# Row projections of a hybrid decoder step with the activations stationary: 128 tokens against 512 weight columns

## The chip, the cores and the metric

The kernel runs on one core of one Trainium2 chip. The metric is device time in microseconds, and smaller is better. TensorE is called PE in the profile, VectorE DVE, ScalarE ACT, GpSimd POOL, and SyncE SP; SP issues the large loads here. PEld is PE's weight load, the step that puts the stationary operand into the array.

## The reference

The program is one inference step of a two-layer decoder. It works on 512 prompt tokens and 64 sample tokens (8 sequences of 8), which share all weights, so the kernel treats them as one matrix of 576 tokens with 1024 features. Cut to what matters here, one layer does this:

```python
h = rms_norm(x, norm1_g) @ w_in                     # (T, 1024) @ (1024, N_IN)
q, k, v, qi, ki, wi, gq, gk, gv, ga, gr, gate_a, gate_b = jnp.split(h, offs, axis=-1)
q = partial_rope(rms_norm(q.reshape(B, T, 8, 64), q_g), pos, 16)
k = partial_rope(rms_norm(k.reshape(B, T, 4, 64), k_g), pos, 16)
qi = partial_rope(qi.reshape(B, T, 4, 64), pos, 16)
ki = partial_rope(rms_norm(ki, kidx_g)[:, :, None, :], pos, 16)[:, :, 0, :]
log_a = jax.nn.log_sigmoid((ga @ gla_wa2 + gla_ba)) / 16
attn_o = dsa_attention(q, qi, wi, pos, ki, topk, ...)   # index scores, top-k, attention over the chosen keys
gla_o, state = gla_recurrence(gq, gk, gv, log_a, s0)    # gated linear attention
x = merge_and_ffn(x, attn_o, gla_o, gr, gate_a, gate_b, ...)
```

The columns of the parts are q 512, k 256, v 256, qi 256, ki 64, wi 4, gq 256, gk 256, gv 512, ga 16, gr 512 and two gates of 1024. Everything is float32.

## The kernel before

**Numbers.** A float32 product is made of three passes in the 32-bit format fp32r. Each operand is split into a high part, which is a rounded copy, and a low part, which is the difference. The product is hi·hi + hi·lo + lo·hi, summed in PSUM. The activations `x_t` (features on partitions, 576 tokens along the row, 8 k tiles) are split into `in_hi` by ACT and `in_lo` by DVE (L2497). The norm's gain goes in there; its 1/rms is applied when a product leaves PSUM.

**Panels.** The weights come in panels of 128 columns by 1024 rows, 512 KB. SP loads them into a ring `w_raw` of three, three panels ahead (`load_panel`). ACT copies a panel to `w_hi` (L1889), and POOL subtracts to get `w_lo` (L1790); both have two buffers, and both wait until PE has finished the panel before the last. On PE (`part`) the weights are stationary and the activations move as two halves of 288 columns. A panel has 8 k tiles of 6 matmuls, 48 in all (L1352). Its output, 128 features by 576 tokens, fills two of the four banks of `prod`, so the next panel has the other two.

**Rows.** Attention and the gated linear attention need q, k, v, the index parts and gv with tokens on partitions (`q_rows`, `kv_rows`, `gv_rows`). These are 15 of the panels of each layer: 4 q, 2 k, 2 v, 2 qi, misc (ga, ki and wi together) and 4 gv; the list `STAGED` names their kinds. For each, ACT copies the product from PSUM to `stage` (L1972). After the first k tile of the next panel, PE turns it: four transposes of 128 tokens (L1465) and one of the 64 sample tokens (L1468) into two banks of `aux`. DVE takes them from there and multiplies them by `r_rows`, the 1/rms of each token (L2530 for q, with its heads put into another order, L2545 and L2553 for the rest). For misc, DVE first takes the 16 rows of ga out of PSUM into `ga_t` (L2307).

**The order.** A class `Plan` writes one list of steps. Every engine walks this list and does what is its own of each step, so its queue stands in that order. In `build_layer` the panels q to misc come first. The normalisations `qn` of q, k and the index keys (one step for each part and each of the five token tiles) are woven in after k tiles 3 and 6 of the panels from k to the first qi. In a `qn` step ACT squares, DVE sums (L2562), ACT forms the root, and DVE scales, applies the gain and rotates (L2258 to L2270). Then come gq and gk, with the items "z" (the decay projection from `ga_t`, ten small products, L1479), "z_min" (ACT's passes for the log-sigmoid) and "decay" woven in by `woven`; then gv with the first index scores and the top-k rounds, and then gr, the gates, the output projections and the feed-forward part, whose products are made by a scheme of seven block products for eight.

**The ends of a layer.** The last panels of layer 1 (`down`) are added to `x_t` by DVE (L2349 scales, L2351 adds). The first panel of layer 2 follows on PE directly.

**The start.** SP loads the x tiles, the gains and then three panels. ACT squares the rows of x and forms `r_rows` from them (L1871 to L1880) before it does anything else. Then it copies the first weights and makes the first `in_hi`. 

```python
for p in range(base, first["gq"]):
    self.start(p)
    for i in range(KD):
        self.add("part", p, i)
        if i == 0 and p > base:
            self.row(p - 1)
        if first["k"] <= p < first["qi"] + 1 and i in (3, 6) and len(normed) > NTILE:
            self.extra_step(normed.pop(0)[0])
```

## Time and profile before

| what | value |
|---|---|
| device time, three runs | 1836.33 us (median), 1833.85, 1837.96 |
| span of the profiled execution | 1837.1 us (no other time of that execution is given) |
| busy share of the span | PE 96%, PEld 92%, DVE 59%, ACT 43%, POOL 43% |
| HBM traffic | 149 MB, 81 GB/s over the span |
| panels | 79 per layer |

Times in the rows are in us from the start of the span unless marked ns. The busy time of a group of matmuls adds up durations that overlap, since the next matmul begins before the last has left the array; so starts are compared here rather than durations. In a timeline, "x4" is a run of four instructions of one line and kind, and a bracket tells how long the engine idled before it and who released it. A granted clock (PEclk) of 1.00 is TensorE's full speed.

### The profile page before, as it was taken

The numbers are of one execution on the slowest core, as the hardware profiler recorded it, in microseconds if no ns is written. First come the engines' busy times: TensorE is split into PE (matmuls) and PEld (weight loads), VectorE is DVE, ScalarE is ACT, GpSimd is POOL, SyncE is SP. The second block draws the span as 40 slices with busy tenths as digits, with TensorE's granted clock in tenths as the row PEclk, the third lists the DMA queues.
The fourth block names the chain that finished last, engine by engine and source line by source line (L and its number), as shares of the span: only waits on it lengthen the run. The fifth ranks groups of instructions, "written<-read, shape, count | busy, mean of one in ns | idle before, by whom it ended". The sixth has DMA issues, their size and how long they took to land.

```text
span 1837.1 us, 34731 instructions
## 1 busy us (share of the span) xinstructions
PE 1764.5 (96%) x13422; PEld 1685.4 (92%) x13422; DVE 1090.8 (59%) x2154; ACT 793.2 (43%) x1515; POOL 785.9 (43%) x508
## 2 busy tenths in 40 slices
PE   7998999999999999999999999999999999999998
PEld 7997888788999999999999878877899999999998
DVE  4655786355587537637536658744556874474463
ACT  4443214465466426426433422145645663363352
POOL 2322443342447447536333333425234563574452
PEclk9999999999999999999999999999999999999999
DMA  5232225214223413313222222342143234233122
GB/s 154 70 87 58 52 73 143 70 36 115 81 81 93 115 58 102 110 50 87 61 70 70 72 74 60 82 126 60 44 119 104 59 93 115 69 94 104 51 63 78
DMA packets 285711, 151.53 MB, mean 82 GB/s; under 512 B 17831, under 2 KB 284139, under 8 KB 285547
## 3 DMA queue, kind: packets, MB, share of 16 engines
q1 hardware_dynamic: 285546, 149.30, 29.7%
q8 instruction: 108, 1.77, 0.4%
q14 instruction: 57, 0.46, 0.1%
HBM read 141.89 MB, written 7.37 MB: 81 GB/s over the span
## 4 chain that ended last, share of the span: by engine, by line
PE 75%; DVE 15%; issue 3%; ACT 3%; SPq 2%; DMA 1%; POOL 0%; DVEq 0%; ACTq 0%; POOLq 0%
PE prod L1352 41%; PE prod L1406 8%; PE prod L1408 8%; PE prod L1407 8%; DVE scores L2710 2%; DVE top L2708 1%; PE aux L1765 1%; PE aux L1753 1%; PE aux L1465 1%; SPq L1179 1%; DVE in_lo L2247 1%; SPq L1185 1%; PE aux L1526 1%; PE aux L1728 1%; DVE aux L2480 1%
## 5 line engine op out<-in xcount | busy, mean ns | idle before, releaser
L1790 POOL TENSOR_TENSOR w_lo<-w_raw,w_hi 128x1024 fp32r<-128x1024 f32 (+1 forms) x158 | 370.8, 2347 | 757.6 <-ACT w_hi L1889 753.1
L1352 PE MATMUL prod<-in_hi,w_hi 128*128 128x288 f32 x1504 | 345.0, 311 | 12.8 <-DVE in_lo L2247 7.8
L1352 PE MATMUL prod<-in_lo,w_hi 128*128 128x288 f32 x1504 | 327.4, 300 | 0.0
L1352 PE MATMUL prod<-in_hi,w_lo 128*128 128x288 f32 x1504 | 326.1, 299 | 0.0
L1352 PEld LDWEIGHTS prod<-in_hi,w_hi 128*128 128x128 f32 x1504 | 244.8, 193 | 33.0 <-issue 24.6
L1889 ACT ACTIVATE w_hi<-w_raw 128x1024 fp32r<-128x1024 f32 (+1 forms) x158 | 163.1, 1032 | 246.1 <-PE prod L1352 245.8
L1352 PEld LDWEIGHTS prod<-in_lo,w_hi 128*128 128x128 f32 x1504 | 247.4, 193 | 0.0
L1352 PEld LDWEIGHTS prod<-in_hi,w_lo 128*128 128x128 f32 x1504 | 247.2, 192 | 0.0
L1406 PE MATMUL prod<-t_hi,ff_hi 128*128 128x288 f32 x704 | 208.7, 296 | 1.5 <-ACT in_sum L1941 0.7
L1352 PE MATMUL prod<-mid_hi,w_hi 128*128 128x288 f32 x960 | 207.6, 298 | 2.0 <-DVE mid_lo L2247 2.0
L1407 PE MATMUL prod<-t_lo,ff_hi 128*128 128x288 f32 x704 | 207.8, 295 | 0.0
L1408 PE MATMUL prod<-t_hi,ff_lo 128*128 128x288 f32 x704 | 207.1, 294 | 0.0
L1352 PE MATMUL prod<-mid_lo,w_hi 128*128 128x288 f32 x960 | 206.4, 296 | 0.0
L1352 PE MATMUL prod<-mid_hi,w_lo 128*128 128x288 f32 x960 | 206.3, 296 | 0.0
L1802 POOL TENSOR_TENSOR ff_lo<-ff_sum,ff_hi 128x512 fp32r<-128x512 f32 x88 | 127.4, 1451 | 80.6 <-ACT ff_hi L1937 80.6
L1352 PEld LDWEIGHTS prod<-mid_hi,w_hi 128*128 128x128 f32 x960 | 153.7, 188 | 3.5 <-DVE mid_lo L2247 3.5
L1406 PE MATMUL prod<-in_hi,ff_hi 128*128 128x288 f32 x528 | 156.4, 296 | 0.4 <-issue 0.4
L1408 PE MATMUL prod<-in_hi,ff_lo 128*128 128x288 f32 x528 | 155.3, 294 | 0.0
L1407 PE MATMUL prod<-in_lo,ff_hi 128*128 128x288 f32 x528 | 155.2, 294 | 0.0
L1352 PEld LDWEIGHTS prod<-mid_hi,w_lo 128*128 128x128 f32 x960 | 154.0, 188 | 0.0
L1352 PEld LDWEIGHTS prod<-mid_lo,w_hi 128*128 128x128 f32 x960 | 153.8, 188 | 0.0
L1406 PEld LDWEIGHTS prod<-t_hi,ff_hi 128*128 128x128 f32 x704 | 131.9, 187 | 3.2 <-issue 2.0
(316 smaller groups left out, 3213.5 us busy)
## 6 DMA issues: line engine op xcount, KB each, us to landing
w_raw<-in_w_in SPq DMA_DIRECT2D x76, 512.0 KB, 3.8
ff_gate<-in_w_ffn_gu SPq DMA_DIRECT2D x44, 512.0 KB, 5.2
ff_up<-in_w_ffn_gu SPq DMA_DIRECT2D x44, 512.0 KB, 4.0
w_raw<-in_w_ffn_down SPq DMA_DIRECT2D x32, 512.0 KB, 4.1
w_raw<-in_w_o SPq DMA_DIRECT2D x16, 512.0 KB, 3.9
w_raw<-in_w_ffn_down SPq DMA_DIRECT2D x16, 384.0 KB, 3.4
k_pages<-in_cache_k SPq DMA_DIRECT2D x32, 128.0 KB, 2.0
v_pages<-in_cache_v SPq DMA_DIRECT2D x32, 128.0 KB, 2.0
```

The costliest lines, as they stand in the source:

```text
L1179: return e.value_load(pages[0:1, i:i + 1], min_val=0, max_val=N_POOL - 1)
L1185: e.dma_start(dst[:, b % 4, n, :], src.rearrange("a s f -> (a s) f")).then_inc(sem[b % 4], 16)
L1352: ins = e.matmul(slot(g)[:, h, :], w[:, slot_w, i * P:(i + 1) * P], a[:, i, h * HALF:(h + 1) * HALF], start=first, stop=last)
L1406: e.matmul(out, ff_hi[:, q % FF_SLOTS, w], hi, start=first, stop=False, skip_group_check=True)
L1407: e.matmul(out, ff_hi[:, q % FF_SLOTS, w], lo, start=False, stop=False, skip_group_check=True)
L1408: ins = e.matmul(out, ff_lo[:, q % FF_SLOTS, w], hi, start=False, stop=(k == 3), skip_group_check=True)
L1465: ins = e.transpose(aux[:, bx, t * P:(t + 1) * P], stage[:, use % 2, t * P:(t + 1) * P], ident)
L1526: ins = e.matmul(aux[:, bank(key), 0:L], qi_t[rows, h // 2, j * P:(j + 1) * P], ki_t[rows, 0:L], start=True, stop=True)
L1790: e.tensor_tensor(w_lo[:, p % 2, 0:n], w_raw[:, p % RAW_RING, 0:n], w_hi[:, p % 2, 0:n].bitcast(F32), ALU.subtract).then_inc(w_lo_done, 1)
L1802: e.tensor_tensor(ff_lo[:, q % FF_SLOTS, :], ff_weights(name, b), ff_hi[:, q % FF_SLOTS, :].bitcast(F32), ALU.subtract).then_inc(ff_lo_don ...
L1889: e.activation(w_hi[:, p % 2, 0:n], w_raw[:, p % RAW_RING, 0:n], ACT.Copy).then_inc(w_hi_done, 1)
L2710: e.match_replace(out=buf, in_to_replace=t8[0:buf.shape[0], :], in_values=buf, imm_value=TAKEN).then_inc(dve_step, 1)
```

## The change

Four new kinds of panel take the place of the 15: `rq` (q, 512 columns), `rkv` (k and v, 512), `rqi` (qi, ki, wi and ga, 340) and `rgv` (gv, 512). Each kind has four panels, and each panel holds two k tiles of all the kind's columns. On PE 128 tokens of `in_hi` or `in_lo` are stationary and the weights move. The outputs have tokens on partitions at once. Token tiles 0 to 3 take the four banks of `prod`, all of them for one kind. The 64 sample tokens have their high and low parts side by side in a new operand `s_both` (128 columns), which moves past no extra pass: one matmul of `s_both` against the high weights and one of the 64 high columns alone against the low weights, into a bank of `aux`. The lower half of that bank's partitions is added to the upper half afterwards.

```diff
+ROW_PARTS = {"rq": [(O_Q, ATTN_W, 0)], "rkv": [(O_K, 2 * KV_W, 0)],
+             "rqi": [(O_QI, IDX_ROW_W + IDX_HEADS, 0), (O_GA, RANK, IDX_ROW_W + IDX_HEADS)],
+             "rgv": [(O_GV, GV_W, 0)]}
+ROW_W = {kind: sum(w for _, w, _ in parts) for kind, parts in ROW_PARTS.items()}
+ROWS = tuple(ROW_PARTS)
...
-    for kind, off, n in (("q", O_Q, 4), ("k", O_K, 2), ("v", O_V, 2), ("qi", O_QI, 2)):
+    def rows(kind):
+        return [(kind, i, [("w_in", 2 * i * P, 2, off, w, place) for off, w, place in ROW_PARTS[kind]])
+                for i in range(4)]
+
+    out += rows("rq") + rows("rkv") + rows("rqi")
...
+    out += rows("rgv")
+    for kind, off, n in (("gr", O_GR, 4), ("gta", O_GTA, 8), ("gtb", O_GTB, 8)):
         out += [(kind, i, [("w_in", 0, KD, off + i * P, P, 0)]) for i in range(n)]
```

PE's part of it, and what it waits for (in `part`, a kind of `ROWS` goes to `row_part`):

```diff
+                def row_part(p, i):
+
+                    kind, idx, _ = PANELS[p]
+                    t, kt, width = i % 4, 2 * idx + i // 4, ROW_W[kind]
+                    g, bank_t = plan.groups[p][t // 2], row_bank(p, t)
+                    cols = slice(i // 4 * width, (i // 4 + 1) * width)
+                    hi_w, lo_w = w_hi[:, p % 2, cols], w_lo[:, p % 2, cols]
+                    first, last = kt == 0, kt == KD - 1
+                    if first and g >= 2:
+                        if PANELS[p - 1][0] in ROWS:
+                            e.wait_ge(rows_out[t], row_no(kind) - 1)
+                        elif t % 2 == 0:
+                            e.wait_ge(free(("g", g - 2)), emptied(("g", g - 2)))
+                    if kind == "rq" and t == 0:
+                        e.wait_ge(split_lo, split_no(("norm", 1, kt)) + 1)
+                    tok = token_slice(t)
+                    out = bank_t[:, 0:width]
+                    e.matmul(out, in_hi[:, kt, tok], hi_w, start=first, stop=False)
+                    e.matmul(out, in_hi[:, kt, tok], lo_w, start=False, stop=False)
+                    ins = e.matmul(out, in_lo[:, kt, tok], hi_w, start=False, stop=last)
+                    if last:
+                        ins.then_inc(row_ready[t], 1)
+                    if t < 3:
+                        return
+                    key = ("rs", kind)
+                    if first:
+                        e.wait_ge(free(key), opened(key))
+                    if kind == "rq":
+                        e.wait_ge(sample_lo, nth(kt + 1, KD))
+
+                    e.matmul(aux[:, bank(key), 0:width], s_both[:, kt, :], hi_w, start=first, stop=False,
+                             skip_group_check=True)
+                    ins = e.matmul(aux[0:NS, bank(key), 0:width], s_both[:, kt, 0:NS], lo_w, start=False,
+                                   stop=last, skip_group_check=True)
+                    if last:
+                        ins.then_inc(ready(key), 1)
+                    elif i == KD - 1:
+                        ins.then_inc(row_part_done, 1)
```

The outputs leave PSUM scaled: tiles 2 and 3 by ACT, which also copies the lower half of the sample bank, and tiles 0 and 1 by DVE, which adds the sample halves and scales them. ACT:

```diff
+                        if kind_p in ROWS:
+                            if kind_p == "rq":
+                                e.wait_ge(r_rows_done, nth(1, 1))
+                                if layer:
+                                    e.wait_ge(stored, nth(0, 16 * 3 * NTILE))
+                            for t in (2, 3):
+                                e.wait_ge(row_ready[t], row_no(kind_p))
+                                for src, dst in row_dests(kind_p, t):
+                                    ins = e.activation(dst, src(row_bank(p, t)), ACT.Copy, scale=r_rows[:, t:t + 1])
+                                ins.then_inc(rows_out[t], 1)
+                            key = ("rs", kind_p)
+                            dst = stage_slot(("fold", kind_p))
                             e.wait_ge(ready(key), filled(key))
-                            if kind_p == "misc":
-                                e.wait_ge(ga_done, nth(1, 1))
-                            e.activation(halves(dst), src, ACT.Copy).then_inc(staged, 1)
+                            e.activation(dst[0:NS, 0:ROW_W[kind_p]], aux[NS:P, bank(key), 0:ROW_W[kind_p]],
+                                         ACT.Copy).then_inc(staged, 1)
```

DVE:

```diff
+                        if kind_p in ROWS:
+                            if kind_p == "rq" and layer:
+                                e.wait_ge(stored, nth(0, 16 * 3 * NTILE))
+                            for t in (0, 1):
+                                e.wait_ge(row_ready[t], row_no(kind_p))
+                                for ps, dst in row_dests(kind_p, t):
+                                    ins = e.tensor_scalar(dst, ps(row_bank(p, t)), r_rows[:, t:t + 1], None, ALU.mult)
+                                ins.then_inc(rows_out[t], 1)
+                            key = ("rs", kind_p)
+                            use = stage_no(("fold", kind_p))
+                            e.wait_ge(staged, use + 1)
+                            for ps, dst in row_dests(kind_p, 4):
+                                ins = e.tensor_tensor(dst, ps(aux[0:NS, bank(key), :]), ps(stage[0:NS, use % 2, :]), ALU.add)
+                            ins.then_inc(free(key), 1)
+                            e.wait_ge(free(key), emptied(key))
+                            dests = [dst for _, dst in row_dests(kind_p, 4)]
+                            if kind_p == "rq":
+                                dests = [q_rows[0:NS, 4, 0:ATTN_W]]
+                            for dst in dests:
+                                ins = e.tensor_scalar(dst, dst, r_rows[0:NS, 4:5], None, ALU.mult)
+                            ins.then_inc(rows_out[4], 1)
```

The staging, the `row` steps with their transposes and DVE's work on them are gone, and so is ga from PSUM; in its place a step `gaT` transposes the 16 columns of ga in five parts, with one copy for the prompt and one for the samples. The `z` items come one item later. The norms' places move too:

```diff
         for p in range(base, first["gq"]):
             self.start(p)
+            if p == 0:
+                self.add("xstat")
             for i in range(KD):
                 self.add("part", p, i)
-                if i == 0 and p > base:
-                    self.row(p - 1)
-                if first["k"] <= p < first["qi"] + 1 and i in (3, 6) and len(normed) > NTILE:
+                if p < first["rqi"]:
+                    due = 2 * NTILE
+                else:
+                    due = NTILE
+                if p >= first["rkv"] and i in (2, 6) and len(normed) > due:
                     self.extra_step(normed.pop(0)[0])
-            if p == base:
+            if p == base + 1:
                 self.rstd(1)
             self.finish(p)
         assert len(normed) == NTILE
 
-        items = [[], normed[0] + [("z",)], [("z_min",)] + normed[1], normed[2], [("decay",)], [("decay_ref",)] + normed[3],
+        items = [[], normed[0] + [("gaT",)], [("z",)] + normed[1], [("z_min",)] + normed[2], [("decay",)],
+                 [("decay_ref",)] + normed[3],
                  normed[4], [("qkT", 0)], [("qkT", 1), ("decay_exp",)], [("qn_end",), ("qkT", 2)], [("qkT", 3)],
                  [("qkT", 4)]]
-        self.woven(range(first["gq"], first["gv"]), items)
...
+                    elif kind == "gaT":
+                        for i in range(2):
+                            e.wait_ge(free(("gaT", i)), opened(("gaT", i)))
+                            for t in range(4 * i, min(4 * i + 4, NTILE)):
+                                n = tile_rows(t)
+                                e.wait_ge(rows_out[t], row_no("rqi"))
+                                ins = e.transpose(aux[0:RANK, bank(("gaT", i)), t % 4 * P:t % 4 * P + n],
+                                                  wga_rows[0:n, t, IDX_HEADS:WGA_W], ident[0:n, 0:n])
+                            ins.then_inc(ready(("gaT", i)), 1)
```

`s_both` is made with the splits for the first norm, by one small instruction more on ACT and one on DVE for each k tile:

```diff
+                        if norm == 1:
+                            e.activation(s_both[:, kt, 0:NS], x_t[:, kt, SEQ:NT], ACT.Copy,
+                                         scale=gains[:, layer, gain:gain + 1]).then_inc(sample_hi, 1)
...
+                        if norm == 1:
+                            e.wait_ge(sample_hi, nth(kt + 1, KD))
+                            e.scalar_tensor_tensor(out=s_both[:, kt, NS:2 * NS], in0=x_t[:, kt, SEQ:NT], scalar=scale,
+                                                   in1=s_both[:, kt, 0:NS].bitcast(F32), op0=ALU.mult,
+                                                   op1=ALU.subtract).then_inc(sample_lo, 1)
```

ACT and POOL wait for the panel before the last by a function `panel_done`, which for the first three panels of a kind is a semaphore of its own, and they work on `panel_cols(p)` columns (1024, in `rqi` 680). A panel of `rqi` is loaded by two DMAs. The squares of x and `r_rows` are now a step `xstat`, which stands in ACT's queue behind the first splits and the first two weight copies, unchanged in itself; `rstd(1)` follows panel 1 in place of panel 0. The loads of the start come in another order:

```diff
             for t in range(NTILE):
                 src = A["x_prompt"][0, t * P:(t + 1) * P, :] if t < 4 else A["x_sample"].rearrange("b s d -> (b s) d")
                 e.dma_start(x_rows[0:tile_rows(t), t, :], src).then_inc(x_loaded[t], 16)
-                if t == 3:
+                if t == 0:
                     load_gains(0)
-            for p in range(RAW_RING):
+                if t == 1:
+                    load_panel(0)
+            for p in range(1, RAW_RING):
                 load_panel(p)
```

## Rows read from the trace of the kernel before

**Rows 1.** Page, part 1: busy us, share of the span, instructions, by engine

```profile
PE 1764.5 (96%) x13422; PEld 1685.4 (92%) x13422; DVE 1090.8 (59%) x2154; ACT 793.2 (43%) x1515; POOL 785.9 (43%) x508
```

**Rows 2.** Page, part 4: the chain that ended last, by engine

```profile
PE 75%; DVE 15%; issue 3%; ACT 3%; SPq 2%; DMA 1%; POOL 0%; DVEq 0%; ACTq 0%; POOLq 0%
```

**Rows 3.** Timeline of PE, two panel boundaries: start us, us, operation

```profile
44.59 0.66 PE L1465 MATMUL aux<-cst,stage 128*128 128x128 f32 x4
...
45.11 0.52 PE L1352 MATMUL prod<-in_hi,w_hi 128*128 128x288 f32 x2
...
51.04 0.42 PE L1352 MATMUL prod<-in_lo,w_hi 128*128 128x288 f32 x2
51.30 0.43 PE L1352 MATMUL prod<-in_hi,w_lo 128*128 128x288 f32 x2
51.73 0.65 PE L1465 MATMUL aux<-cst,stage 128*128 128x128 f32 x4
```

**Rows 4.** Waits of PE: who waited for whom, us in total, times, longest

```profile
PE aux L1465 <- ACT stage L1972: 3.6, 6, 0.9
```

**Rows 5.** Timeline of PE in attention: products of 384 and 512 columns

```profile
383.31 0.33 PE L1368 MATMUL aux<-k_lo,q_split 128*128 128x384 f32 x1
383.48 0.43 PE L1352 MATMUL prod<-in_hi,w_hi 128*128 128x288 f32 x2
...
411.14 0.39 PE L1368 MATMUL aux<-k_lo,q_split 128*128 128x512 f32 x1
411.37 0.42 PE L1352 MATMUL prod<-in_hi,w_hi 128*128 128x288 f32 x2
```

**Rows 6.** Timeline of PE: outputs of 64 partitions, a row transpose and score sums

```profile
45.08 0.27 PE L1468 MATMUL aux<-cst,stage 128*64 128x128 f32 x1
...
184.38 0.43 PE L1352 MATMUL prod<-in_hi,w_lo 128*128 128x288 f32 x2
184.74 1.29 PE L1563 MATMUL aux<-s_heads,cst 128*64 128x320 f32 x4
185.96 0.53 PE L1352 MATMUL prod<-in_hi,w_hi 128*128 128x288 f32 x2
```

**Rows 7.** One line's instructions (ns min/median/max); timeline of DVE

```profile
L1889 ACT ACTIVATE w_hi<-w_raw x158: 839/1052/1067, 14.6 to 1820.5; 128x1024 fp32r<-128x1024 f32 x142, 128x768 fp32r<-128x768 f32 x16
...
59.64 0.69 DVE L2545 TENSOR_TENSOR kv_rows<-aux,r_rows 128x512 f32<-128x512 f32 x1 [0.42 <-PE aux L1465]
```

**Rows 8.** Timelines of DVE and POOL, normalisation of q beside a weight subtraction

```profile
59.85 2.41 POOL L1790 TENSOR_TENSOR w_lo<-w_raw,w_hi 128x1024 fp32r<-128x1024 f32 x1 [4.73 <-ACT w_hi L1889]
...
61.35 1.47 DVE L2258 TENSOR_TENSOR q_rows<-q_rows,sums 128x512 f32<-128x512 f32 x1
...
65.10 0.68 DVE L2258 TENSOR_TENSOR q_rows<-q_rows,sums 128x512 f32<-128x512 f32 x1
```

**Rows 9.** Timelines of PE and DVE where gq begins

```profile
103.53 0.50 PE L1352 MATMUL prod<-in_hi,w_hi 128*128 128x288 f32 x2
...
105.28 2.56 PE L1479 MATMUL aux<-wa,ga_t 17*128 17x256 f32 x10
...
107.56 0.22 DVE L2270 TENSOR_TENSOR kv_rows<-rope,rope 64x64 f32<-64x64 f32 x1
```

**Rows 10.** Timelines of PE and DVE where the second layer begins

```profile
921.71 0.43 PE L1352 MATMUL prod<-in_hi,w_hi 128*128 128x288 f32 x2
...
922.84 0.76 DVE L2351 TENSOR_TENSOR x_t<-prod,x_t 128x576 f32<-128x576 f32 x1
```

**Rows 11.** Chain in order of time, the last two steps of the start

```profile
16.44 2.28 DVE in_lo L2497
...
18.86 1.30 PE prod L1352 x4
```

**Rows 12.** Stretches: us, busy of PE, PEld, DVE, ACT, POOL, clock, DMA share, GB/s

```profile
0.00:17.40 17.40, 7.28 (x41) 6.29 (x41) 7.21 (x14) 10.50 (x19) 1.86 (x5) 1.00 0.96 268
17.40:24.30 6.90, 5.44 (x23) 5.47 (x24) 6.90 (x7) 4.54 (x7) 2.98 (x2) 0.51 0.42 114
```

223 lines of the change are left out of this document (98 added, 125 removed).

## The prediction, made before the changed kernel was run

> **What bounds the kernel now.** I read the page first. TensorE is busy for 1764.5 us of the span and holds 75% of the chain that ended last; DVE, next, holds 15% [rows 1, 2]. So a microsecond comes off the kernel only where TensorE's stream gets shorter or where a wait of that stream goes. The timeline of PE then shows what one input panel costs: from the row transposes at 44.59 us to the next ones at 51.73 us are 7.14 us, of which the block of five transposes takes 0.52 (45.11 less 44.59) and 48 matmuls of 288 columns the rest, 0.138 each on the mean and 0.133 from start to start inside the stream (two in 0.265) [rows 3]. The durations of 0.3 us are no guide: they overlap. The list of waits shows that those transposes wait for ACT's staging copy 3.6 us in all, six times [rows 4]. The other engines idle beside this stream most of the time.
>
> **The change, part by part.** All times come from the profiled execution, whose span is 1837.1 us; that is 0.8 above the median of the three runs shown, so I take the difference off the median.
>
> *The stream.* Removed per layer: 15 panels (4 q, 2 k, 2 v, 2 index, misc, 4 gv) of 7.14 us, 107.1 us, transposes included. Added per layer: four kinds of four panels with 8 x 3 prompt matmuls and 2 x 2 sample matmuls, 28 each; twelve panels are 512 columns wide, the four of the index kind 340. The trace has three-pass operands at 512 columns in the attention logits: the second of such a pair starts 0.23 us before the next matmul (411.14 to 411.37), with 384 columns 0.17 us [rows 5]. I take 0.23 (ends 0.22 and 0.24, since the rows are rounded) and for 340 columns, between 0.133 and 0.17, 0.155. That is 336 x 0.23 + 112 x 0.155 = 94.6 us. Gain 12.5 per layer, **24.9 us** in all. With the low ends (0.22, 0.133) it is 37, with the high ones (0.24, 0.17) 15. The number of columns hardly changes (207,360 against 210,112 per layer); what goes is the fixed part of 272 matmuls and the 75 transposes.
>
> *Waits that go:* the 3.6 us of rows 4, since neither the staging nor the misc panel's product is between two panels any more. **3.6 us.**
>
> *The narrow stationary.* In each half panel the last sample matmul has 64 stationary columns, 64 such instructions in all. A plain matmul of that shape is costly to enter and leave: the last two of 288 columns before the score sums take 0.36 instead of 0.265, and the four of these with the return take 1.22, so about 0.09 each way [rows 6]. The fifth row transpose has 64 stationary columns too and costs nothing: its start is 0.49 after the first of four and the next matmul starts 0.03 later [rows 6]. The dtype of the new ones is that of neither. I take nothing, as they stand amid equal matmuls like the transposes, and keep 64 x 0.18 = 11.5 us as the other end. The Trainium skill (TensorEngine Tiling (Array Packing), Key Properties) says that changing the tiling mode drains TensorE, which speaks against this change; the first pair of rows 6 agrees with it and by it the sum would be 11.5 us worse. The same skill (PSUM — Partial Sum Buffer, on the zero region) says that float32r matmuls force the full column group, by which nothing would be drained; no run so far shows it.
>
> *Ga by transposes.* Five transposes per layer, 0.13 each by the block of rows 3: **+1.1 us**. The z products wait for DVE's copies of them. After the index kind ends (0), ACT evicts its two tiles and folds (to 1.0), casts the next weights (1.05, to 2.1), and POOL subtracts (2.4, to 4.5) [rows 7, 8]. DVE meanwhile has the last k tile's norm. Such an operation of two SBUF operands takes 1.47 us while POOL works on w_lo and 0.68 without it [rows 8], so the norm ends about 1.5 after POOL, at 6.0; it now ends 4.3 us after the row block (103.53 to 107.8) with a smaller load [rows 9]. The copies add 0.9 (the 128x512 move from PSUM is 0.69 [rows 7]), to 7.0. TensorE is there after five steps of 0.8 and the transposes, at 4.7, where the z block now begins without a wait [rows 9]. Stall 2.3 per layer, **+4.6** (0 to 8). What is late next is the chain of ACT's three passes over z; the decay products that need it stand two items later, six steps and the z block of 2.5 us behind [rows 9], and I count nothing for them.
>
> *Evictions.* All four banks of prod belong to one kind, so the next kind needs them at once. Tile 0's bank is complete 2.5 us before the kind ends, tile 3's 0.45, and the next kind comes to them in turn every 0.69 us. DVE's 0.69 (q's turned heads in two instructions of half the width) and the same on ACT, by estimate, fit: nothing on the path if DVE is free. It is: from one q norm's product to the next's are 3.75 us, of which 0.8 is what POOL's work costs it [rows 8]; with that in part of them, some 3.4 each, five q norms need 17 of the 25.8 us (112 x 0.23) of the kv kind. If DVE were late by a norm (3 us), each of eight boundaries could cost that.
>
> *Weights.* The w_hi copy (1.05) stands in ACT's queue behind evictions and the squares of the norms, and POOL's 2.4 follows [rows 7, 8]. A 512 panel lasts 6.4 us, so the copy may begin 2.9 us late; an index panel (680 columns in place of 1024) lasts 4.3 with 0.7 + 1.6 us of work, and may begin 2.0 us late. By walking ACT's queue I find only the third index panel late, by 0.6 per layer: **+1.2** (0 to 5). SP's queue issues four DMAs more per layer, three panels ahead, and waits for POOL there now: hidden.
>
> *The second layer's first panel* opens banks of both last down panels. The last addition to x begins at 922.84 and takes 0.76, to 923.60; the stream begins at 921.71 and comes to the third tile 1.38 later, at 923.09 [rows 10]: **+0.5**.
>
> *The start.* The x tiles' last landing waits for 512 KB of weights in front, 2 us at the rate of rows 12; against that ACT's squares and the first cast are out of the way and POOL's first w_lo is done, which now holds DVE's first in_lo for 2.28 us until TensorE starts at 18.86 [rows 11]. With the loads at 268 GB/s [rows 12] I get 18.0; until 24.3 the granted clock is 0.51, the 1.2 of TensorE's two levels of 1.2 and 2.4 GHz [rows 12], so half of it counts: **-0.5**. The squares now delay the third panel's weights until 35.5, where TensorE arrives at 35.4: nothing. Ends -1.5 and +1.5.
>
> Sum: -24.9 - 3.6 - 0.5 + 1.1 + 4.6 + 1.2 + 0.5 = **-21.6 us**, 1815.5 in the profile's terms, 1814.7 on the median.
>
> **Rivals.**
> - *Drain.* The narrow stationary costs like the plain one: 1814.7 + 11.5 = 1826. For it the score-sum rows, against it the transposes [rows 6]. Chance 0.17.
> - *Clean handover.* Neither the z wait nor the index weights bite, and a 340-column matmul costs nearer 0.145: 4.6 + 1.2 + 2.2 us more gain, 1807. For it: the walks above take every queue at its latest. Chance 0.13.
> - *Weights late, the other side.* ACT stands in the norms' handshakes with DVE, so that each weight cast of the kv and index kinds, 16 panels, starts behind them. It decides from 1.35 us of wait per panel (21.6/16); if the slack of 2.9 and 2.0 is exceeded by 3, TensorE loses 48 us: 1863. For it: the norms now come in two per 6.4 us instead of 7.14, and each costs up to 3.75 beside POOL's work [rows 8]. Against it: five q norms in 25.8 us leave room. Chance 0.04.
> - *Moved wait.* The stream is shorter but the gv stage is held by DVE's top-k and index work, and the stalls give all back: about 1836. DVE holds 15% of the chain [rows 2], though it idles between those steps. Chance 0.03.
> - The change does what it says; I see no way in which it would not.
>
> **Numbers.** Forecast 0.63, 1814.7, its own range 1808 to 1822. The range of 1804 to 1828 takes in the fast end of the stream partly, the clean handover and the drain, and leaves out the two last rivals. A stretch at half clock more or less, such as the 6.9 us of rows 12, costs half its length, 3.5 us, and lies inside it. A measurement of this kernel tells 0.2% (3.7 us) from no change. Faster by more: 0.63 + 0.17 + 0.13 = 0.93; within: 0.03; slower: 0.04.
>
> **What would show it.** In the profile after: 512-column groups at L1352's successor with 0.23 us from start to start; no staging or row transposes, a wait of about 2 us before the z products on DVE's ga copies, a short one on w_lo in the index panels, one before the third tile of the second layer. It would be wrong if the narrow matmuls' neighbours lie 0.3 us apart, if PE waits for POOL's w_lo at most panels, or if the four kinds' stages are not 77 and 17 us of stream per layer.

## The result, and the profile after

The changed kernel takes 1826.91 us, the median of six runs (1825.65 to 1833.26), beside 1836.39 for the kernel before in six (1833.85 to 1837.96). The ratio is 0.9955, with a 95% interval of 0.994 to 0.997. Two more sets of runs were made on other chips: 1830.41 beside 1835.52 (0.9976, 0.9962 to 0.9989) and 1830.42 beside 1836.36 (0.9963, 0.9949 to 0.9976). So the change gains 5 to 9.5 us. Forecast were 21.6, and 1814.7: the sign was right, the size not.

The profiled execution has a span of 1831.5 us; it is the slowest of the six (1833.26), so it shows less of the gain than the medians. The page (parts 1 and 4) answers to [rows 1, 2]:

```profile
PE 1747.9 (95%) x12738; PEld 1638.1 (89%) x12738; DVE 1099.6 (60%) x2146; ACT 796.6 (43%) x1535; POOL 784.0 (43%) x510
...
PE 73%; DVE 14%; ACT 4%; issue 3%; SPq 3%; DMA 2%; POOL 1%; DVEq 0%; ACTq 0%; POOLq 0%
```

PE is busy 16.6 us less (1764.5 less 1747.9), but the span is only 5.6 shorter. So 11.0 us of what was taken out of PE's work came back as time in which PE is not busy, and part of its busy time is work at a lower clock. The waits of PE (who waited for whom: us in total, times, longest) show new names:

```profile
PE aux L1785 <- DMA k_pages<-in_cache_k: 5.7, 3, 3.2
...
PE prod L1400 <- POOL w_lo L1891: 5.0, 5, 1.6
PE aux L1693 <- ACT gk_rows L2263: 4.5, 2, 2.2
...
PE aux L1581 <- DVE ga_t L2644: 3.2, 2, 1.6
...
PE aux L1589 <- DVE la L2676: 2.6, 2, 1.3
...
PE prod L1456 <- DVE wga_rows L2426: 1.0, 2, 0.5
```

In the kernel before, the first of them stood so:

```profile
PE aux L1683 <- DMA k_pages<-in_cache_k: 1.8, 2, 1.3
```

Where they fall is seen when the start of each kind's first product is read from PE's timeline. The table gives the length of each stretch in the two profiled executions:

| stretch | before, layer 1 | after | before, layer 2 | after |
|---|---|---|---|---|
| q (first product at 18.86, 18.89) | 31.91 | 29.91 | 32.51 | 28.63 |
| k and v | 28.96 | 25.55 | 28.96 | 25.55 |
| index parts and ga | 21.44 | 20.55 | 21.44 | 20.52 |
| gq and gk | 39.68 | 43.66 | 39.70 | 45.16 |
| gv | 49.19 | 45.17 | 47.65 | 45.26 |
| gr to the next layer, or the last down panels | 731.67 | 735.89 | 435.38 | 436.86 |

A kind's stream promises 4 x (7.14 - 6.39) = 3.0 us where 512 columns move, and the three such kinds gain 2.0 to 4.0. The index kind gains 0.9 where 3 x 7.14 less 4 x 4.39, 3.9, were in the stream. gq and gk, whose own panels are unchanged, take 4.0 and 5.5 us longer, and behind gr the kernel takes 4.2 and 1.5 us longer.

**The stream.** PE's timeline at full clock, with the narrow stationary of the samples in the middle, and inside an index panel:

```profile
30.90 0.39 PE L1413 MATMUL aux<-w_hi,s_both 128*128 128x512 f32 x1
31.13 0.40 PE L1415 MATMUL aux<-w_lo,s_both 128*64 128x512 f32 x1
31.36 0.39 PE L1400 MATMUL prod<-w_hi,in_hi 128*128 128x512 f32 x1
```

```profile
85.12 0.32 PE L1401 MATMUL prod<-w_lo,in_hi 128*128 128x340 f32 x1
85.27 0.32 PE L1402 MATMUL prod<-w_hi,in_lo 128*128 128x340 f32 x1
```

512 columns take 0.23 from start to start [rows 5], 340 take 0.15, and the one with 64 stationary columns takes 0.23 like its neighbours. A panel of 512 columns lasts 6.39 us, an index panel without waits 4.39, so a layer's stream is 12 x 6.39 + 4 x 4.39 = 94.2 us; forecast were 94.6.

**The index kind and gq.** PE's timeline again; a bracket is the idle time before, and who ended it:

```profile
84.86 0.42 PE L1400 MATMUL prod<-w_hi,in_hi 128*128 128x340 f32 x1 [1.62 <-POOL w_lo L1891]
...
89.80 0.43 PE L1400 MATMUL prod<-w_hi,in_hi 128*128 128x340 f32 x1 [0.34 <-POOL w_lo L1891]
...
94.90 0.50 PE L1456 MATMUL prod<-in_hi,w_hi 128*128 128x288 f32 x2 [0.50 <-DVE wga_rows L2426]
...
97.36 0.75 PE L1568 MATMUL aux<-cst,wga_rows 128*16 128x128 f32 x5
...
101.48 2.53 PE L1581 MATMUL aux<-wa,ga_t 17*128 17x256 f32 x10 [1.58 <-DVE ga_t L2644]
...
111.87 0.35 PE L1589 MATMUL aux<-cst,la 128*128 128x128 f32 x1 [1.34 <-DVE la L2676]
```

The same five waits stand in layer 2, within 0.07 us. The third is that of gq for the bank that DVE empties last. The last two, before z and before the decay products, stand where the kernel before has none.

**Why the weights are late.** First ACT, then POOL, then DVE around the beginning of the index kind (74.35):

```profile
78.26 0.42 ACT L2170 ACTIVATE sq_rows<-kv_rows 128x256 f32<-128x256 f32 x1 [2.21 <-DVE kv_rows L2439]
...
82.28 0.76 ACT L1992 ACTIVATE w_hi<-w_raw 128x680 fp32r<-128x680 f32 x1
```

```profile
76.13 1.66 POOL L1891 TENSOR_TENSOR w_lo<-w_raw,w_hi 128x680 fp32r<-128x680 f32 x1 [5.17 <-ACT w_hi L1992]
```

```profile
76.15 1.92 DVE L2439 TENSOR_SCALAR kv_rows<-kv_rows,r_rows 64x512 f32<-64x512 f32 x1
```

DVE scales the sample rows of k and v from 76.15 to 78.07, beside POOL's w_lo. Only then does ACT square the first tile of k (78.26): the first norm of a part waits for all five tiles of it, the samples' too. DVE is behind by one norm from there. ACT's queue holds the copy for the third index panel behind that norm, so it begins at 82.28, POOL follows it, and PE waits until 84.86. The same instruction costs a quarter elsewhere (ns, min/median/max):

```profile
L2439 DVE TENSOR_SCALAR kv_rows<-kv_rows,r_rows x2: 1921/1922/1924, 76.1 to 975.6; 64x512 f32<-64x512 f32 x2
...
L2439 DVE TENSOR_SCALAR gv_rows<-gv_rows,r_rows x2: 478/478/479, 185.5 to 1086.5; 64x512 f32<-64x512 f32 x2
```

For gv, with as many elements and with POOL idle when it starts (185.5; POOL's next work begins at 185.81), it takes 0.48; for k and v 1.92. The Trainium skill (SBUF — State Buffer, Who interferes with whom) says that only the port pair shared by DVE and GpSimd causes contention, and that it is an exclusive lock. The trace agrees: the two began 0.02 us apart, POOL's ended at its usual length (77.79), and DVE's 0.28 after it.

**Why z and the decay are late.** DVE in the gq stage, ACT at the end of its passes over z, and DVE in the kernel before:

```profile
97.21 1.90 DVE L2373 TENSOR_TENSOR kv_rows<-kv_rows,sums 64x256 f32<-64x256 f32 x1
...
100.30 0.93 DVE L2644 COPY ga_t<-aux 16x512 f32<-16x512 f32 x2
107.66 0.22 DVE L2653 TENSOR_REDUCE sums<-sq_rows 128x1 f32<-128x64 f32 x1 [6.43 <-ACT sq_rows L2170]
...
109.08 0.76 DVE L2443 SCALAR_TENSOR_TENSOR gq<-prod,rstd 128x576 f32<-128x576 f32 x1
109.75 1.86 DVE L2676 SCALAR_TENSOR_TENSOR la<-aux,la 128x512 f32<-128x512 f32 x3
```

```profile
107.32 0.24 ACT L2170 ACTIVATE sq_rows<-q_rows 128x64 f32<-128x64 f32 x1
```

```profile
110.52 1.87 DVE L2585 SCALAR_TENSOR_TENSOR la<-aux,la 128x512 f32<-128x512 f32 x3 [2.75 <-ACT la L2085]
```

The copies of ga stand behind the last norm of k, which POOL stretches again (1.90 for 0.41), so z waits 1.58. Then `z_min`, which writes `la`, has slipped behind two things on DVE, since z comes one item later and ahead of its item's norm: that norm, whose square ACT makes only after its passes over z, and gq's own product. DVE sits idle until that square, does the norm from 107.66, and takes gq's product at 109.08 without any wait for PE. So `la` comes at 109.75, 3.8 us after ACT began its last pass over z (105.95). In the kernel before it came 0.74 after (110.52 and 109.78), with the norm and gq's product behind it. PE waits 1.34 us before the decay products.

**The start.** ACT, DVE and PE, answering to [rows 11]:

```profile
17.03 0.78 ACT L2116 ACTIVATE in_hi<-x_t,gains 128x576 fp32r<-128x576 f32 x1 [6.34 <-DVE gains L2345]
...
24.29 1.05 ACT L1992 ACTIVATE w_hi<-w_raw 128x1024 fp32r<-128x1024 f32 x1
```

```profile
14.76 2.09 DVE L2352 COPY x_t<-aux 128x512 f32<-128x512 f32 x4 [0.58 <-PE aux L1375]
```

```profile
18.89 0.76 PE L1400 MATMUL prod<-w_hi,in_hi 128*128 128x512 f32 x1 [2.42 <-DVE in_lo L2626]
...
28.04 0.50 PE L1400 MATMUL prod<-w_hi,in_hi 128*128 128x512 f32 x1 [1.05 <-POOL w_lo L1891]
```

The last copies of x end at 16.85 (14.2 before): the 512 KB in front cost 2.7 us. The squares are out of the way and the first `in_lo` takes 0.82 instead of 2.28, so PE starts at 18.89, as before. But the second copy of weights now waits for eight splits of 0.92 us each, with the samples' own copies among them (0.68 before), and starts at 24.29 (20.90 before), and PE loses 1.05 at the second panel.

**The clock.** Where the z products stood idle and where the decay starts, the granted clock falls (us, busy of the five engines, clock, DMA share, GB/s):

```profile
100.00:103.90 3.90, 2.42 (x10) 1.59 (x10) 1.12 (x4) 1.01 (x2) 0.00 (x0) 1.00 0.42 129
103.90:107.40 3.50, 3.50 (x15) 3.46 (x15) 0.00 (x0) 3.44 (x9) 0.00 (x0) 0.51 0.00 0
1001.60:1008.50 6.90, 6.90 (x23) 5.18 (x23) 0.00 (x0) 4.61 (x10) 0.00 (x0) 0.51 0.00 0
```

Both stretches follow the 1.6 us wait; the kernel before has 1.00 in its z block (105.2 to 108.7). In the seven profiles that have the wait before z, such a stretch begins 0.6 to 3.6 us behind each of the 14 waits. The waits for weights in the index kind of layer 2 are as long (1.6), and none comes within 17 us of them. In all, 44.8 us of this execution are at 1.2 GHz instead of 2.4, against 38.0 before; in the two other profiles of the changed kernel it is 37.6 and 54.1.

### The profile page after: what moved, and what is told of

It reads as the page before. It is cut to its first block, busy times and chain, and to the rows that moved or that the text cites. A ratio compares the mean times of both kernels' runs of the same rounds, so it can differ in the third digit from the quotient of the medians.

```text
span 1831.5 us, 33285 instructions
## 1 busy us (share of the span) xinstructions
PE 1747.9 (95%) x12738; PEld 1638.1 (89%) x12738; DVE 1099.6 (60%) x2146; ACT 796.6 (43%) x1535; POOL 784.0 (43%) x510
## 4 chain that ended last, share of the span: by engine, by line
PE 73%; DVE 14%; ACT 4%; issue 3%; SPq 3%; DMA 2%; POOL 1%; DVEq 0%; ACTq 0%; POOLq 0%
PE prod L1456 32%; PE prod L1510 8%; PE prod L1511 8%; PE prod L1512 8%; PE prod L1400 2%; PE prod L1401 2%; PE prod L1402 2%; PE aux L1867 1%; PE aux L1855 1%; SPq L1244 1%; DVE scores L2801 1%; DVE in_lo L2362 1%; SPq L1250 1%; DVE top L2799 1%; PE aux L1628 1%
## 5 line engine op out<-in xcount | busy, mean ns | idle before, releaser
L1891 POOL TENSOR_TENSOR w_lo<-w_raw,w_hi 128x1024 fp32r<-128x1024 f32 (+2 forms) x160 | 370.1, 2313 | 752.7 <-ACT w_hi L1992 748.2
L1992 ACT ACTIVATE w_hi<-w_raw 128x1024 fp32r<-128x1024 f32 (+2 forms) x160 | 163.2, 1020 | 276.4 <-PE prod L1456 244.9
L1456 PE MATMUL prod<-in_hi,w_hi 128*128 128x288 f32 x1024 | 238.8, 315 | 8.8 <-DVE in_lo L2362 7.8
L1456 PE MATMUL prod<-in_lo,w_hi 128*128 128x288 f32 x1024 | 224.4, 302 | 0.0
L1456 PE MATMUL prod<-in_hi,w_lo 128*128 128x288 f32 x1024 | 224.1, 301 | 0.0
L1456 PEld LDWEIGHTS prod<-in_hi,w_hi 128*128 128x128 f32 x1024 | 169.4, 195 | 25.7 <-issue 17.6
L1456 PEld LDWEIGHTS prod<-in_lo,w_hi 128*128 128x128 f32 x1024 | 170.0, 195 | 0.0
L1456 PEld LDWEIGHTS prod<-in_hi,w_lo 128*128 128x128 f32 x1024 | 169.9, 194 | 0.0
```

Of the source, the lines that this page charges most:

```text
L1456: ins = e.matmul(slot(g)[:, h, :], w[:, slot_w, i * P:(i + 1) * P], a[:, i, h * HALF:(h + 1) * HALF], start=first, stop=last)
L1891: e.tensor_tensor(w_lo[:, p % 2, 0:n], w_raw[:, p % RAW_RING, 0:n], w_hi[:, p % 2, 0:n].bitcast(F32), ALU.subtract).then_inc(w_lo_done, 1)
L1992: e.activation(w_hi[:, p % 2, 0:n], w_raw[:, p % RAW_RING, 0:n], ACT.Copy).then_inc(w_hi_done, 1)
```

## The experiments

**The changed kernel again, twice** (no edit).

> The changed kernel again. Its six runs so far lie in two groups, 1825.7 to 1827.3 and 1832.4 to 1833.3, with mean granted clocks of 0.989 to 0.992 and 0.988. Theory A (the change gained some 16 us of stream and small waits, and half-clock stretches more or less make the groups): in the runs of this kernel a time about 5.5 us longer goes with a mean clock lower by 0.003, and the profile up to the start of gr again shows some 11 us less over both layers. Rival B (the stages behind gr wait for something that does not start earlier, such as the loads of the pages in SP's queue): the profile again has over 2 us of PE's wait on k_pages in layer 1, and the time stays near 1826 to 1833 whatever the clock.

> The changed kernel once more, on the chip of the two others, as their yardstick: 1824 to 1832, with a granted clock about 0.002 below that of the kernel before.

Measured: 1830.41 us in twelve runs and 1830.42 in six, with mean clocks of 0.9869 and 0.9865 beside 0.9895 and 0.9884 for the kernel before on the same chips. There are no two groups, but a spread of 1823 to 1835 that goes with the clock: the run at 0.992 took 1823.42, those at 0.983 and 0.984 took 1835.42 and 1835.23. Over all 24 runs of this kernel a line through time and clock falls by 1.0 us for 0.001, less than I had expected (5.5 for 0.003). By that line 0.002 to 0.0026 less clock go with 2 to 2.6 us. If all of a half-clock stretch cost half its length, 0.001 would be 1.8 us (3.7 us at 1.2 GHz); so part of it seems to fall where PE would have waited anyway. PE's wait on k_pages was 4.0 us in the second profile, 3.3 of them in layer 1, as the rival had it. As far as the start of gr, the two profiles lie 2.5 and 5.0 us ahead in layer 1, and 9.2 and 8.3 over both layers, not 11.

**The start undone**, wholly and in part. The first kernel puts the squares in front again and takes the old order of loads, the second the order alone:

```diff
-                if t == 0:
+                if t == 3:
                     load_gains(0)
-                if t == 1:
-                    load_panel(0)
-            for p in range(1, RAW_RING):
+            for p in range(RAW_RING):
                 load_panel(p)
```

> The squares of x stand in front again and the loads are in the old order; all else is the changed kernel. Theory A (the new start gains nothing: the x tiles land later behind 512 KB of weights, and the second w_hi copy stands behind 8 small sample splits): PE's first product at about 18.9 us or earlier, no wait on w_lo before panel 1, or less than 1.05 us, and the rq kind ends 0 to 2 us earlier. Rival (the start was a gain of 0.5 us, as forecast): the end of the rq kind comes 0.5 us or more later, since ACT's splits begin behind 5 us of squares.

> Only the order of the first loads is the old one, the squares stay behind the splits. Theory A: the last x tile's copies end 2 us earlier (14.3 instead of 16.8), the first w_hi copy (1.05) comes then, and POOL's first w_lo (2.35) takes DVE's first in_lo with it, so PE starts at about 18.0 and the rq kind ends 1 to 2 us earlier than 48.8. Rival: the weights, now last, land after 16.8 and PE starts later than 18.9.

Measured: 1827.64 and 1827.26 us, on the chip where the changed kernel took 1830.41. With both undone PE starts at 18.87 and the k kind at 47.73. With the order alone undone:

```profile
14.11 2.10 DVE L2624 SCALAR_TENSOR_TENSOR in_lo<-x_t,gains,in_hi 128x576 fp32r<-128x576 f32 x1 [0.99 <-ACT in_hi L2114]
```

```profile
16.35 0.76 PE L1398 MATMUL prod<-w_hi,in_hi 128*128 128x512 f32 x1 [3.69 <-DVE in_lo L2624]
```

PE starts at 16.35, with POOL's lock on the first `in_lo` (2.10) as expected but 1.6 earlier than expected, and the k kind begins at 45.40. There is no wait at the second panel. The start moves from one profile to the next, and other kernels of this document share it. With the new start (eight profiles) the k kind begins at 47.2 to 49.3, 48.3 on the mean; with the order alone undone (three) at 44.8 to 46.8, 45.7 on the mean. So the new order of the loads costs some 2.6 us, and moving the squares gains about 2 by the one profile without it (47.7). Whether both together gain or lose anything cannot be told. The medians are 3 us shorter, within the spread.

**The norms of k one panel later.**

```diff
-                if p >= first["rkv"] and i in (2, 6) and len(normed) > due:
+                if p >= first["rkv"] and p != first["rqi"] and i in (2, 6) and len(normed) > due:
```

> The norms of k leave the first index panel free and stand in the last three (five steps for six places). Theory A (w_lo of the third and fourth index panel is late, 1.62 and 0.34 us per layer, because ACT's copy stands behind norms of k which wait for DVE): the third panel's wait falls from 1.62 to under 0.5 us, the kind is 1 to 2 us shorter per layer, unless the norms crowd the fourth panel, and the time falls by 2 to 3 us. Rival B (what is gained before gr is lost behind it): the kind is shorter, but the time is within 1 us of the changed kernel's. Rival D (the number of norms in the kind counts, not their place): the wait moves to the last panel and to the first of gq and stays 2 us in all.

Measured: 1835.34 us, as slow as the kernel before (1.0, 0.9987 to 1.0013). The index kind lasts 21.6 us instead of 20.5, and gq and gk 47.2. The waits of PE:

```profile
PE prod L1456 <- DVE wga_rows L2426: 8.2, 2, 4.1
```

The waits for weights in the index kind are gone, as expected, but the gain did not come. The norms now crowd the kind's end, and DVE empties its last bank 4.1 us late per layer, where it was 0.5; the kind is 17.56 of stream and this wait. The rival that only the number of norms counts had the place but not the size, and the wait on `la` is 5.7 us as well. The mean clock is 0.984, as low as in any kernel.

**gaT ahead of the norm.**

```diff
-        items = [[], normed[0] + [("gaT",)], [("z",)] + normed[1], ...
+        items = [[], [("gaT",)] + normed[0], [("z",)] + normed[1], ...
```

> The gaT step stands before the first norm of its item, in place of behind it. Theory A (the z products wait 1.6 us per layer because DVE's copies of ga stand behind the last norm of k, which POOL's subtraction stretches): that wait goes, the ten z products start 1.6 us earlier relative to gq's start, and, since ACT's three passes over z start earlier too, the wait before the decay products (1.3 us per layer) does not grow. Gain 2 x 1.6 = 3.2 us, up to 5 if the half-clock stretch that follows that wait in each profile so far (at 103.95 and 1001.66) does not come. Rival (ACT's and DVE's norm chain sets the stage): the wait on la grows by what the z wait loses, and gq plus gk stay at about 43.7 us (layer 1) in time corrected for the clock.

Measured: 1829.83 us (0.9958, 0.9945 to 0.9971), no change that can be told. The changed kernel did not run on this chip, so the ratio to the kernel before is what compares. The wait before z is gone, and the wait on `la` has grown (DVE's timeline, then PE's waits):

```profile
107.43 0.76 DVE L2443 SCALAR_TENSOR_TENSOR gq<-prod,rstd 128x576 f32<-128x576 f32 x1
108.10 1.86 DVE L2676 SCALAR_TENSOR_TENSOR la<-aux,la 128x512 f32<-128x512 f32 x3
```

```profile
PE aux L1589 <- DVE la L2676: 5.7, 2, 2.9
```

The two waits were 3.2 + 2.6 us and are 0 + 5.7, so the rival holds in its waits. It is not a plain move, though. `la` again comes 3.8 us after ACT began its last pass over z, and with z earlier the decay products begin 15.3 us behind gq's start in both layers, where they began 17.0 and 18.5 behind. PE comes to them earlier still, since no half-clock stretch lies between z and them. So it seems that in the changed kernel the stretch fell on time that PE would otherwise have waited for `la`. gq and gk last 42.0 and 45.1 us (43.7 and 45.2 before the edit); in layer 2 a stretch at half clock comes right behind the wait on `la` instead.

**The sample rows scaled as they leave PSUM** (loops and semaphores are left out of the cut).

```diff
+    ins = e.tensor_scalar(dst, ps(aux[0:NS, bank(key), :]), r_rows[0:NS, 4:5], None, ALU.mult)
     e.wait_ge(staged, use + 1)
-    ins = e.tensor_tensor(dst, ps(aux[0:NS, bank(key), :]), ps(stage[0:NS, use % 2, :]), ALU.add)
-    ins = e.tensor_scalar(dst, dst, r_rows[0:NS, 4:5], None, ALU.mult)
+    ins = e.scalar_tensor_tensor(out=dst, in0=ps(stage[0:NS, use % 2, :]), scalar=r_rows[0:NS, 4:5],
+                                 in1=dst, op0=ALU.mult, op1=ALU.add)
```

> The sample rows are scaled as they leave PSUM, before ACT's fold is there, and the fold is scaled and added in one step; the scaling of SBUF by SBUF (1.92 us beside POOL's w_lo, 76.15 to 78.07 in the profile) is gone, as many instructions on DVE. Theory A (that stretched instruction holds the next norm, and the norm holds ACT's copy for the third index panel): the first norm of k starts 1.5 to 1.9 us earlier, the wait before the third index panel falls from 1.62 to about 0, the index kind lasts 18.0 to 19.0 us in place of 20.5; 2 to 4 us in all. Rival (the norms themselves are too slow for panels of 4.4 us): the wait moves to the fourth panel and the kind stays above 20 us.

Measured: 1826.82 us (0.9956, 0.9943 to 0.9969). DVE, and PE at the third and fourth index panel:

```profile
73.33 0.74 DVE L2433 TENSOR_SCALAR kv_rows<-aux,r_rows 64x512 f32<-64x512 f32 x1 [1.02 <-PE aux L1416]
74.31 0.74 DVE L2439 SCALAR_TENSOR_TENSOR kv_rows<-stage,r_rows,kv_rows 64x512 f32<-64x512 f32 x1 [0.23 <-ACT stage L2085]
```

```profile
82.28 0.43 PE L1401 MATMUL prod<-w_hi,in_hi 128*128 128x340 f32 x1 [0.34 <-POOL w_lo L1892]
...
87.22 0.43 PE L1401 MATMUL prod<-w_hi,in_hi 128*128 128x340 f32 x1 [0.34 <-POOL w_lo L1892]
```

The last step ends at 75.05, where POOL's work has just begun (74.92), and the wait at the third panel falls from 1.62 to 0.34 us. The index kind lasts 19.16 us, 1.4 less in each layer. The last step ends 1.9 us behind the kind before it instead of 3.7: 1.44 of these 1.8 are the stretching beside POOL, and the rest is that the scaling no longer waits for ACT's copy. So the stretched scaling was the main cause of the late weights, and 0.34 at two panels is what is left. In the time of the whole kernel this edit alone does not show: its ratio is that of the changed kernel (0.9955 to 0.9976 on other chips).

**The narrow stationary made wide.**

```diff
-    aux[0:NS, bank(key), 0:width], s_both[:, kt, 0:NS], lo_w
+    aux[:, bank(key), 0:width], s_both[:, kt, :], lo_w
```

> The second sample matmul has all 128 columns of s_both stationary in place of 64, so lo x lo of the samples is computed too and no matmul of these kinds is narrower than the others. Theory A (the 64-column stationary costs nothing: 0.23 us from its start to the next in the changed kernel's timeline, like its neighbours): the start-to-start times are the same within 0.01 us and the time is the changed kernel's within its noise of 4 us. Rival (drain, 0.18 us for each of 64): 11 us faster.

```profile
30.98 0.39 PE L1415 MATMUL aux<-w_lo,s_both 128*128 128x512 f32 x1
31.21 0.39 PE L1400 MATMUL prod<-w_hi,in_hi 128*128 128x512 f32 x1
```

Measured: 1828.03 us (0.9954, 0.9939 to 0.9968), and 0.23 from start to start, as before the edit. The drain rival is out. Of the two rules that the prediction weighed, that of the Trainium skill (PSUM — Partial Sum Buffer, The four PSUM rules) on float32r matmuls forcing the full column group agrees with this; the one on draining (TensorEngine Tiling (Array Packing), Key Properties) does not show at an fp32r matmul with 64 stationary columns among ones with 128.

**Four edits together, the decay one item later.** The sample rows scaled first, the old order of loads, gaT ahead, and:

```diff
-   [("z_min",)] + normed[2], [("decay",)], [("decay_ref",)] + normed[3], normed[4],
+   [("z_min",)] + normed[2], normed[3], [("decay",)], [("decay_ref",)] + normed[4],
```

> Four edits together: the loads of the start in the old order, gaT before the norm, the sample rows scaled first, and the decay products one item later (it now waits 1.3 us per layer for la). Theory A (each handover costs what its wait shows, and they are on the path): 2.5 (start) + 3.2 (z) + 2.6 (la) + 3.5 (index weights) = 11.8 us less than the changed kernel, of which a part may be given back as half-clock stretches; 1815 to 1820. Rival B (what comes before gr does not carry to the end): earlier by 8 us or more at gr of layer 1, but less than half of it left at the gates' second kind, and 1823 or more in the end.

Measured: 1831.42 us (0.997, 0.9959 to 0.9981), not the 1815 to 1820 expected, and not by the rival's way either: at gr of layer 1 it is 7.1 us ahead of the kernel before, not 8 or more. At the start of gq in layer 2 this kernel is 15.4 us ahead of the one before, but gq and gk last 46.7 and 45.5 us, 7 and 6 more than before:

```profile
PE aux L1602 <- ACT q_t L2178: 6.0, 2, 3.0
```

The decay's own work on DVE (`decay_ref` and what follows) now ends later, the norm behind it too, and behind that norm stand ACT's weight copy and its first copy of q, which PE waits for: 3.0 us per layer. A step moved back to where its input is ready pushed back the chain behind it.

**z_min ahead of gq's product**, and with it the best version.

```diff
-        items = [[], normed[0] + [("gaT",)], [("z",)] + normed[1], [("z_min",)] + normed[2], [("decay",)],
+        items = [[], [("gaT",)] + normed[0], [("z",), ("z_min",)] + normed[1], normed[2], [("decay",)],
```

> The changed kernel with two moves in the gq stage: gaT ahead of the norm of its item, and z_min directly behind z, so that on DVE it stands ahead of gq's product. Theory A (with gaT ahead alone the wait on la grew from 1.3 to 2.9 us per layer, since DVE's z_min stands behind gq's own product, which waits for PE): the waits before z and before the decay products, 2.9 us per layer in the changed kernel, are both under 0.5, and gq plus gk last about 40.8 us in layer 1 in place of 43.7; 1806 to 1809 us in time corrected for the clock means a gain of 5.8. Rival (something third takes over, ACT's passes or q_t's transposes): gq plus gk stay over 42.5 us.

> zmin_early with the old order of the first loads and the sample rows scaled as they leave PSUM. Theory A (the handovers are on the path): 5.8 (z, la) + 2.5 (start) + 2.8 (index weights) = 11 us less than the changed kernel on the same chip; some 1817 to 1820, less what goes back as half-clock stretches (4 to 7 us at the clocks seen so far). Rival B (gains before gr do not reach the end): under 3 us less than the changed kernel.

Measured: 1823.17 us (0.993, 0.9917 to 0.9943) and, with the old load order and the scaling in PSUM, 1819.06 us (0.9908, 0.9895 to 0.992), where the changed kernel took 1830.42 on the same chip. DVE's order is turned round:

```profile
96.41 0.93 DVE L2644 COPY ga_t<-aux 16x512 f32<-16x512 f32 x2 [1.43 <-PE aux L1568]
...
103.49 1.87 DVE L2676 SCALAR_TENSOR_TENSOR la<-aux,la 128x512 f32<-128x512 f32 x3 [4.42 <-ACT la L2200]
...
106.81 0.76 DVE L2443 SCALAR_TENSOR_TENSOR gq<-prod,rstd 128x576 f32<-128x576 f32 x1
```

```profile
PE aux L1604 <- ACT q_t L2180: 2.5, 2, 1.3
```

The waits before z and the decay are gone (5.8 us), and one of 1.3 us per layer on ACT's copy of q has come (2.5); gq and gk last 40.4 us in both layers. So the two moves in the plan gain 3.3 us by waits, and 7.2 by the runs. In the profiles gq and gk shrink by 3.3 and 4.8 us, of which the waits are 1.7 per layer; the rest fits half of the stretches of 3.4 and 6.8 us at half clock, of which this profile has none in the stage. The mean clock is 0.9892 instead of 0.9865, which at 1.0 us for 0.001 is 2.7 us. The best version lasts 11.4 us less than the changed kernel, against 11 expected, at a clock of 0.987. Theory A stands in its total: the handovers together cost about what their waits show, and what was taken away before gr did reach the end. Its check by time corrected for the clock (1806 to 1809) did not hold: the span less half of its 33.3 us at half clock is 1802.2, and the changed kernel's three profiles give 1801.8 to 1809.1 by the same sum. PE's waits for the weights of the row kinds, 5.0 us in the changed kernel, are down to this:

```profile
PE prod L1399 <- POOL w_lo L1890: 1.4, 4, 0.3
```

## Why the prediction was wrong in its size

The bound was read rightly, and so was the stream. The terms, both layers together, as the profiled execution has them:

| term | forecast | measured |
|---|---|---|
| stream, with the row transposes | -24.9 | -25.8 (2 x (107.1 - 94.2)) |
| waits for staging | -3.6 | -3.6 |
| narrow stationary | 0 | 0 |
| transposes of ga | +1.1 | +1.3 (2 x 0.65) |
| wait before z | +4.6 | +3.2 |
| wait before the decay products | 0 | +2.6 |
| weights of the index kind | +1.2 | +3.9 |
| gq's wait for the last bank | 0 | +1.0 |
| layer 2's first banks | +0.5 | +0.6 |
| the start | -0.5 | +1.1 (48.80 less 47.73), not clear of the spread |
| page loads (5.7 less 1.8) | 0 | +3.9, open |
| half clock (44.8 less 38.0, halved) | 0 | at most +3.4 |

The sum of the last column is -8.4. The profiles differ by 5.6, the medians by 9.5, 5.1 and 5.9. Of the 2.8 between, 1.5 are PE's wait on `gk_rows` (4.5 for 3.0; it is 3.0 in the two other profiles of this kernel), and the rest has no place. The last term and the wait on `la` overlap in part, by the run with gaT ahead.

- **"I count nothing for them"**, of the decay products, is the step that failed most plainly. I asked whether ACT's passes over z would be in time, and not what `z_min` would stand behind on DVE once z was an item later. It stands behind a norm and gq's product. Before, it began at 110.52 and gq's product at 113.85. That cost 2.6 us, and moving it back, with gaT, took 7.2 us off the kernel, part of it by the clock.
- **"By walking ACT's queue I find only the third index panel late, by 0.6"**: the place was right, the size 1.62 and 0.34 more at the fourth. The prediction had POOL's lock for the norms, 0.8 each, and left out the scaling of the sample rows, 1.44 longer beside POOL, right in front of ACT's square of the first tile of k.
- **"Nothing on the path if DVE is free. It is"**: at the end of the index kind it was late by 0.5 us, behind a norm of which one small step (L2381, 128x32) took 2.39 us beside POOL's w_lo at 90.77 and 0.18 at 87.80. At the other boundaries of a kind PE has no wait, as forecast.
- **The start**: the squares behind the splits gain about 2 us, and the loads' order loses some 2.6. I had the landing 2 us later (it was 2.7) and did not see that the second cast stands behind eight splits with an extra step each.
- **The z wait**: the mechanism was the one forecast (the norm stretched by POOL, 1.90 us), 1.6 in place of 2.3.
- **The clock** was held to be a matter of chance inside the range. It was lower in the changed kernel on both chips where it was compared, and as high as before (0.9892, 0.9884) in the kernel without the two waits. In the profiles every wait before z has a stretch behind it, and where z waits no more, the kernel with z_min ahead has no stretch in gq and gk, and the best version one of 3.4 us, in layer 2. That this wait brings the stretch is the likeliest reading; but the best version, which lacks both waits too, had 0.987, so the mean clock is not settled by it.

Of the rivals, the drain is out (the wide matmul); its price of 0.09 for each way was read too boldly, since rows 6 show the way in (0.36 for 0.265) but do not part the way back from the four matmuls themselves. Weights late was right in its mechanism, but at 4 of the 16 panels it named, and by less than 2 us each; its 48 us needed every panel. Even the best version stops at 17.3 us, short of the 21.6, with 0.3 at some panels, a clock 0.0014 lower than before and the page loads left.

The page loads stay open. SP issues them behind the end of the sample recurrence: 286.35 against 290.74 before, only 4.4 us earlier where PE was 6 ahead, and PE waited 3.18 for them at 311.11. From 286.35 to 314.8 SP issues them one behind the other with little idle time, so that its own pace sets when the last come. PE's wait was 3.6 to 6.2 us in every profile with the new panels and 1.8 before. From gr of layer 1 to the next layer each of these twelve profiles took 732.9 to 738.0 us, where the kernel before took 731.7, and in 2.2 to 3.7 of that PE waited for the pages (0.5 before); behind gr of layer 2 no such loss shows (740.3 to 747.1 to the end, 745.2 before). The sum had no term for this: it took what PE gains ahead of gr to be kept. That these loads keep their time while PE gets ahead is the reading of these rows; no run changed their order.

## What to carry to other kernels

When a plan is written by hand, a step that is moved has to be looked up in every queue: what stands between its old and its new place on each engine, and whether one of those waits for something that comes later still. Shorter panels leave the helpers less time, so an instruction that a shared port stretches fourfold is cheap in one stage and sets the next one's start in another; reading it from PSUM, before POOL's work began, took it off the path here. Two small waits in one stage cost more than their length when the clock falls behind them.

## What was not expected of the hardware

A scaling of 64 x 512 in SBUF took 1.92 us beside a POOL subtraction of 1.66, and 0.48 with POOL idle at its start. In a kernel whose PE is busy 95% of its span, a wait of 1.6 us ahead of the z products was followed by a half-clock stretch of 3.4 or 6.8 us in 14 cases of 14, and waits of the same length ahead of an index panel by none. Over 24 runs of this kernel 0.001 of mean clock goes with 1.0 us.
